# The layer end of a two-layer hybrid recurrent decoder step: three pieces of work issued at other places

## The reference

```python
h = rmsnorm(x, p['norm_w'])
proj = einsum('bld,dn->bln', h, p['w_in'])        # 1024 -> 25 chunks of 128 columns
# S5: a complex scan over time gives y, then
y = gelu(y)
y = y * sigmoid(einsum('blc,cn->bln', y, w_glu))  # the GLU: a 256 x 256 product of y itself
# HGRN2 and GLA: gated chunk scans, outputs normed per head (rmsnorm)
# RetNet: retention scan, output normed per head with its mean taken off (layernorm)
mix = concat([y_s5 * silu(s5_z), y_hg * silu(hg_z), y_gla * silu(gla_z), y_ret * silu(ret_z)])
x = x + einsum('bln,nd->bld', mix, p['w_out'])    # 1024 -> 1024
# after both layers: a final rmsnorm
```

## Time and profile before

| | us |
|---|---|
| median of three runs | 356.77 |
| lowest, highest | 356.39, 358.14 |
| the profiled execution, its own time | 357.73 |
| the profiled execution, its span | 355.9 |
| TensorE busy in the span | 333.9 (94%) |
| VectorE busy | 229.8 (65%) |
| ScalarE busy | 128.3 (36%) |

### The profile page before, as it was taken

One profiled execution on the slowest core, in us unless ns is written; L12 is line 12 of the kernel. 1 busy time (PEld: TensorE's weight loads), 2 busy tenths in 40 slices (PEclk: granted clock), 3 DMA queues, 4 the chain that ended last, 5 costly groups with the idle time before them and its releaser, 6 DMA issues.

```text
span 355.9 us, 6388 instructions
## 1 busy us (share of the span) xinstructions
PE 333.9 (94%) x2546; PEld 282.8 (79%) x2546; DVE 229.8 (65%) x481; ACT 128.3 (36%) x282; POOL 43.9 (12%) x81
## 2 busy tenths in 40 slices
PE   7899998889999999989979999999999999999991
PEld 6588876668889898769957888878888989767990
DVE  2574499986548973585559527596654897358454
ACT  4252001150780103982312620124276010596421
POOL 4028520006000002140000000000500000120000
PEclk9999999999999999899989999999999999989997
DMA  8977631232522401499805473322442433437503
GB/s 282 385 245 258 207 114 61 82 97 87 155 90 97 142 2 31 150 209 362 338 1 173 138 260 97 105 88 88 122 150 65 133 99 112 148 85 151 182 0 122
DMA packets 28012, 50.84 MB, mean 143 GB/s; under 512 B 6288, under 2 KB 6864, under 8 KB 27984
## 3 DMA queue, kind: packets, MB, share of 16 engines
q1 hardware_dynamic: 25968, 44.06, 37.3%
q0 software_dynamic: 1728, 6.29, 7.3%
q10 hardware_dynamic: 288, 0.09, 0.1%
HBM read 46.80 MB, written 3.64 MB: 142 GB/s over the span
## 4 chain that ended last, share of the span: by engine, by line
PE 68%; DVE 13%; ACT 10%; POOL 4%; issue 2%; DMA 1%; DVEq 0%; POOLq 0%; ACTq 0%
PE pr L486 39%; PE pr L759 10%; ACT u L966 4%; DVE att L1319 2%; PE wk L553 2%; DVE h L1051 2%; PE wk L675 2%; PE wk L500 2%; ACT w_lo L1027 2%; POOL lev L1556 2%; PE wk L598 1%; POOL lev L1558 1%; PE wk L566 1%; PE wk L667 1%; PE wk L613 1%
## 5 line engine op out<-in xcount | busy, mean ns | idle before, releaser
L486 PE MATMUL pr<-h,wring 128*128 128x264 f32 x768 | 184.2, 397 | 3.2 <-DVE h L1051 3.2
L486 PEld LDWEIGHTS pr<-h,wring 128*128 128x128 f32 x768 | 146.6, 194 | 31.5 <-issue 5.9
L759 PE MATMUL pr<-a_hi,w_hi 128*128 128x264 f32 x96 | 27.6, 288 | 0.0
L759 PE MATMUL pr<-a_lo,w_hi 128*128 128x264 f32 x96 | 27.2, 283 | 0.0
L759 PE MATMUL pr<-a_hi,w_lo 128*128 128x264 f32 x96 | 27.2, 283 | 0.0
L943 ACT ACTIVATE zs<-pr 128x264 f32<-128x264 f32 x16 | 6.0, 384 | 45.1 <-PE pr L486 45.0
L872 ACT ACTIVATE v<-pr 128x264 f32<-128x264 f32 x12 | 4.7, 388 | 48.2 <-PE pr L486 48.2
L860 ACT ACTIVATE h<-x 128x264 f32<-128x264 f32 x24 | 9.5, 420 | 32.7 <-DVE x L1460 30.6
L1319 DVE COPY_PREDICATED att<-masks,wk 128x512 f32<-128x512 int32 x20 | 17.6, 949 | 1.0
L759 PEld LDWEIGHTS pr<-a_hi,w_hi 128*128 128x128 f32 x96 | 18.1, 188 | 0.1
L759 PEld LDWEIGHTS pr<-a_lo,w_hi 128*128 128x128 f32 x96 | 18.1, 188 | 0.1
(11 more groups left out here) (279 smaller groups left out, 539.9 us busy)
## 6 DMA issues: line engine op xcount, KB each, us to landing
wring<-in_w_in SPq DMA_DIRECT2D x100, 256.0 KB, 3.0
wring<-in_w_out SPq DMA_DIRECT2D x20, 256.0 KB, 3.7
w_hi<-in_w_out POOLq DMA_DIRECT2D x6, 512.0 KB, 4.4
w_lo<-in_w_out POOLq DMA_DIRECT2D x6, 512.0 KB, 8.2
x<-in_xt SPq DMA_DIRECT2D x2, 528.0 KB, 4.6
out_y<-h SPq DMA_DIRECT2D x4, 264.0 KB, 2.1
s5m_t<-in_s5m SPq DMA_DIRECT2D x2, 512.0 KB, 4.9
ss<-in_hg_in SPq DMA_DIRECT2D x2, 512.0 KB, 4.0
```

The source lines that it names most:

```text
L486: mm = nc.tensor.matmul(ring_bank(layer, i)[:, 0:TT], wring[:, slot, n, :], act_in[:, k, :], start=(k == 0), stop=(k == KT - 1))
L759: mm = nc.tensor.matmul(ring_bank(layer, i)[:, 0:TT], w[:, j % WSLOTS, n, :], a[:, k, :], start=(k == 0 and p == 0), stop=(k == KT - 1 and ...
```

## The change

Four pieces, in both layers:

1. On ScalarE, tanh of the S5 gelu is issued ahead of SiLU of chunk 23 (it was behind it). On VectorE, the end of the gelu follows the first `gather_outputs`.
2. The back copies are divided: groups 0 and 1 go to VectorE, as `tensor_scalar` with factor 0.5, ahead of the second `gather_outputs`; groups 2 and 3 stay on ScalarE, behind SiLU of chunk 23. TensorE, and VectorE in `s5_mix`, wait for one more semaphore, `yg_act`.
3. On TensorE the GLU product and the two head means go ahead of chunk 24. On ScalarE tanh of the GLU product and the three negating copies go ahead of SiLU of chunk 24. The banks `pr` follow by a list, `BANK_TURN`, that gives the turns in the new order.
4. On VectorE, `head_gates` of tiles 0 to 3 goes from ahead of `center` to behind the second `square_outputs`.

```diff
+        BANK_TURN = list(range(NCH - 1)) + [NCH, NCH + 1, NCH - 1] + list(range(NCH + 2, USES))
         def ring_free(eng, layer, i):
-            i -= 3
+            i = BANK_TURN.index(i) - 3
             if i < 0:
                 layer, i = layer - 1, i + USES
+            i = BANK_TURN[i]
...
         def ring_bank(layer, i):
-            return pr[(layer * USES + i) % 3]
+            return pr[(layer * USES + BANK_TURN.index(i)) % 3]
...
             def glu_gate(layer):
                 pe.wait_ge(yg_ready, layer + 1)
+                pe.wait_ge(yg_act, layer + 1)
...
                 sample_outputs(layer, 1)
-                project(layer, NCH - 1)
                 glu_gate(layer)
                 ret_means(layer)
+                project(layer, NCH - 1)
                 head_norms(layer)
...
-            def s5_back(layer):
+            def s5_back(layer, groups):
                 act.wait_ge(yb_ready, layer + 1)
...
-                for a in range(4):
+                for a in groups:
...
-                         yg_ready if a == 3 else None)
+                         yg_act if a == groups[-1] else None)
...
                     if i == NCH - 2:
                         for n in range(2):
                             s5_evac(layer, n)
-                    if i == NCH - 1:
                         act.wait_ge(tin_ready, layer + 1)
                         step(fn(yt2, yt2, ACT.Tanh, scale=GELU_C), tanh_ready)
-                        s5_back(layer)
+                    if i == NCH - 1:
+                        s5_back(layer, (2, 3))
+                        act.wait_ge(glu_done, layer + 1)
+                        step(fn(glu[:, :, :], wk[:, 0:2, 0:TT], ACT.Tanh, scale=0.5), glu_tanh)
+                        negated_high(layer)
                     silu(layer, i)
...
-                for n in range(BY_DMA):
-                    act.wait_ge(hi_in[n], 16 * (layer + 1))
-                    step(fn(w_lo[...], w_hi[...], ACT.Copy, scale=-1.0), neg_ready)
-                act.wait_ge(glu_done, layer + 1)
-                step(fn(glu[:, :, :], wk[:, 0:2, 0:TT], ACT.Tanh, scale=0.5), glu_tanh)
                 use_logs()
...
+            def s5_back(layer, groups):        # VectorE
+                settle()
+                yv = yb.rearrange("p (t s k) -> p t s k", t=2, s=4)
+                for a in groups:
+                    for j in range(4):
+                        dst = qrt(yg, a)[:, :, 0:TP].rearrange("p t (k j) -> p t k j", j=SL)[:, :, :, j]
+                        step(ts(dst, qrt(yv, j)[:, :, a, 0:SC], 0.5, None, ALU.mult))
+                    step(ts(qrt(yg, a)[:, :, TP:TT], qrt(yv, 0)[:, :, a, SC:], 0.5, None, ALU.mult),
+                         yg_ready if a == groups[-1] else None)
...
                 s5_gelu(layer)
-                for kind in range(2):
-                    gather_outputs(layer, kind)
+                gather_outputs(layer, 0)
                 s5_gelu_end(layer)
+                s5_back(layer, (0, 1))
+                gather_outputs(layer, 1)
                 gather_outputs(layer, 2)
                 gather_samples(layer)
                 square_outputs(layer, slice(0, 4))
-                head_gates(layer, range(0, 4))
                 center(layer)
                 square_outputs(layer, slice(4, 6))
+                head_gates(layer, range(0, 4))
                 s5_mix(layer)
```

More of the change, by code:

```diff
@@ L280, in build @@
             sem(n) for n in ("gtr_evac", "sin_ready", "y_evac", "tanh_ready", "glu_tanh", "osq_ready", "ors_ready", "lb_act", "lb2_act"))
+        yg_act = sem("yg_act")
         dve_step, h_ready, t_ready, ls_ready, tree_ready, op_ready, lvl_used = (
@@ L967, in s5_back, with negated_high @@
                     step(fn(qrt(yg, a)[:, :, TP:TT], qrt(yv, 0)[:, :, a, SC:], ACT.Copy, scale=0.5),
-                         yg_ready if a == 3 else None)
+                         yg_act if a == groups[-1] else None)
+            def negated_high(layer):
+                for n in range(BY_DMA):
+                    act.wait_ge(hi_in[n], 16 * (layer + 1))
+                    step(fn(w_lo[:, 2 * n:2 * n + 2, :, :], w_hi[:, 2 * n:2 * n + 2, :, :].bitcast(F32), ACT.Copy, scale=-1.0), neg_ready)
             def s5_evac(layer, n):
@@ L1024, in _ @@
                         s5_turned(layer, range(4))
-                for n in range(BY_DMA):
-                    act.wait_ge(hi_in[n], 16 * (layer + 1))
-                    step(fn(w_lo[:, 2 * n:2 * n + 2, :, :], w_hi[:, 2 * n:2 * n + 2, :, :].bitcast(F32), ACT.Copy, scale=-1.0), neg_ready)
-                act.wait_ge(glu_done, layer + 1)
-                step(fn(glu[:, :, :], wk[:, 0:2, 0:TT], ACT.Tanh, scale=0.5), glu_tanh)
                 use_logs()
@@ L1413, in s5_gelu_end @@
                 step(stt(out=yb, in0=yt2, scalar=1.0, in1=yb, op0=ALU.add, op1=ALU.mult), yb_ready)
+            def s5_back(layer, groups):
[7 more added lines that the diff above has]
+                         yg_ready if a == groups[-1] else None)
             def s5_mix(layer):
+                dve.wait_ge(yg_act, layer + 1)
                 dve.wait_ge(glu_tanh, layer + 1)
```

## The result

The changed kernel takes 353.64 us (median of 13 runs, 351.23 to 356.90); the kernel before, in its 13 runs, 356.39 us (354.53 to 358.14). The ratio is 0.9909, 95% interval 0.9884 to 0.9933: 2.4 to 4.1 us faster. Forecast were 356.2 us and a range from 355.0 to 357.3 us. The ratio is that of the means of the fast runs: two executions of the changed kernel, 356.81 and 356.90 us, count as slow and are left out, and with them it is 0.9927.

What follows compares the result with a forecast made beforehand. TensorE, 94% busy, was taken as near its limit, with the first Ln's start deciding the layer end. Ln 0.30 us earlier in each of two layers gives 0.6 us: 356.77 to 356.2 us, range 355.0 to 357.3 us.

Steps and rivals of the forecast that it cites:

- VectorE's share: VectorE's ten back copies take 2.6 us, ending at 138.3 us, before ScalarE's half; they cost nothing.
- TensorE waits 0 to 0.2 us: Sign of being right: before the GLU product TensorE waits this long for `yg`; 0.1 us was expected.
- the same 28 records with the same 1.97 us of slow clock: TensorE's GLU product, means and chunk 24 keep their 8.43 us in the new order, ending at 151.0 us.
- the prediction's second rival: Clock falls once more at TensorE's gaps by the norms and output chunk 0: 1.7 us each, 359.6 us in both layers; 5%.
- The clock falls once less: Rival: the layer end keeps 2.4 GHz, giving 354.2 us for one layer, 352.2 us for both; 10%.
- By itself this gives nothing: Tanh of the gelu moved earlier on ScalarE gains zero before part 2, since no engine on the path uses it.
- The rule on the table load: Before Ln on ScalarE: 1.3 us taken for the load; the skill's extra drain, 2.66 us in all, would mean 358.8 us.
- It does nothing: Rival: `yg` comes 0.4 us or more after 142.48 us and the wait eats the gain, 356.8 us; 14%.
- slower: Outcome slower by more than 1.8 us, through an added slow clock in both layers, a delayed table load or mishap; 8%.
- TensorE's gap at the fourth norm: TensorE's idle time before the fourth head norm, ended by Ln, shrinks from 1.18 to about 0.8 us.
- The three times before span 1.75 us, about one such stretch.: Argument for a varying clock: the earlier kernel's spread of times is about one slow stretch at chunk 24.

Runs made afterwards that it cites:

- the run with the outputs apart: Kernel before, with the first half of the sample outputs moved ahead of the retention outputs; 355.78 us, ratio 1.0002.
- after twice: The changed kernel measured two times without further edit: 353.64 us (ratio 0.9909), then 351.64 us (ratio 0.9868).
- back copies early: Changed kernel with ScalarE's back copies of groups 2 and 3 ahead of SiLU of chunk 23; 351.68 us, ratio 0.9859.
- part 4 undone: Changed kernel with head gates of tiles 0 to 3 back ahead of `center`; 353.39 us, ratio 0.9910.
- no division: Changed kernel with all four groups of back copies on ScalarE, GLU product still ahead of chunk 24; 364.90 us, ratio 1.0228.
- Parts 1 and 2 alone: Changed kernel with chunk 24 back ahead of the GLU product and head gates back ahead of `center`; 352.98 us, ratio 0.9890.
- run without part 3: Changed kernel with chunk 24 back ahead of the GLU product and ScalarE's block behind its SiLU; 355.25 us, ratio 0.9947.
- the combined version: Changed kernel with sample outputs split, copies before SiLU 23, chunk 24 before GLU, third negating copy behind second Exp, head gates before `center` and S5 mix; 350.40 us.
- the three profiles with the two halves 2.5 us apart: First half of sample outputs ahead of retention outputs: in the kernel before (355.78 us), the changed kernel (352.21 us) and the combined version (350.40 us).

## Why the prediction was wrong

The chain through ScalarE was read rightly, the load and Ln too, and so was where the new gap would be. What was wrong is the price of TensorE's stretch ahead of the norms, and with it what the clock is worth.

- **Parts 1 and 2.** The last copy for `yg` ended at 143.00 us and the GLU product started at 143.10 us, 0.23 us after TensorE was free (142.87 us, 1.97 us behind the first sample output as before); the forecast was 0.1 (0 to 0.2). The copies began at 138.91 us, just behind the end of SiLU of chunk 23 and not 0.1 us ahead of it. VectorE's share was hidden, as forecast. That "TensorE waits 0 to 0.2 us" was off by a little; one more place for the copies (ahead of SiLU) takes the wait away.
- **"Then follow the same 28 records with the same 1.97 us of slow clock, 150.91 - 142.48 = 8.43 us."** This is the step that failed, twice over. First, 8.43 us was not TensorE's own work. In the new order the records take 6.30 us at full clock and 8.00 us with a slow stretch, so a slow stretch costs 1.70 us and not 1.97 us (the prediction's second rival had 1.7 us). In the old order they take 6.34 us at full clock and without a wait, so about 8.04 us with a slow stretch, an estimate; the other 0.39 us of the 8.43 was the wait for `yg`. It did not show, because the profile models the ends of matmuls: the row of the GLU product had no idle time, and I took chunk 24 to have ended just before it. The 0.43 us that the stretch is shorter, less 0.13 us more wait for `yg` and 0.10 us more ahead of SiLU of chunk 24 (it starts 0.20 us after the norms, forecast 0.1), turns 0.30 us a layer into 0.54 us (0.04 us of it is the forecast's rounding), the number measured in layer 0, where a slow stretch stood again.
- Second, I carried the slow stretch over as a constant. The forecast treats TensorE's time ahead of the norms as something both orders pay. But in the old order nothing of it was on the path: the chain of the earlier trace rows left TensorE at 138.11 us and came back at 153.59 us. The old order pays 15.86 us with a slow stretch and, from chunk 24 on, the same without one, as the run with the outputs apart shows (13.88 against 13.89 us). The new order pays 15.32 us with it and 13.65 us without it. Since the stretch isn't there in every layer end, the gain is 0.54 us in one and 2.22 us in another.
- **"The clock falls once less" at 10%.** The rival was listed, but as luck, the same for both kernels, and priced against the time of the new order alone. It needed no fewer slow stretches: those that do not come had given the old kernel nothing, and give the new one 1.7 us each. Two layer ends give 1.1 to 4.4 us; the measured 2.75 us between the medians lies in the middle. The table by mean clock says the same of 100 executions. A mean clock doesn't say where a slow stretch stood; in the five profiled executions with the changed kernel's order at the outputs (after twice, back copies early, part 4 undone, and no division with its own idle gap) it stood in five of ten layer ends. How many of them an execution holds stays luck, and so does the exact time within 1.1 to 4.4 us of gain.
- **"By itself this gives nothing" (part 1) and the share of part 3.** The gain was looked for in part 3. The prediction says this of part 1 alone and never prices parts 1 and 2 together; the two expectations that call their zero its forecast say more than it did. Parts 1 and 2 alone give 1.78 us a layer at full clock, part 3 0.43 us. I had computed that Ln moves by 0.30 us because chunk 24 then stands ahead of it, and did not ask what the old TensorE order would do with `yg` early.
- **The rule on the table load.** The load took 1.28 us behind a SiLU that had just read a bank, started 0.02 us after it, and Ln followed at once: no drain of 1.38 us. The Trainium skill (ScalarE: Activation LUTs, What ACT_TABLE_LOAD costs) gives 1283 ns for the load itself, and the trace agrees; what it adds for the drain doesn't show here.
- **"It does nothing" and "slower".** Neither came. The gaps of 0.85 us brought no slow stretch. A wait of 4.06 us at `yg` did: the slower rival's mechanism is real at that size.
- **TensorE's gap at the fourth norm** shrank from 1.18 to 0.85 us (forecast 0.8), with Ln at 153.00 us (forecast 152.85, in an execution that ran 0.39 us late, so 0.24 us sooner than forecast). TensorE waited for no weight transfer in that profile, and `head_mix` not for the head gates, as forecast.
- **"The three times before span 1.75 us, about one such stretch."** The spread of the kernel before isn't the clock. At one and the same mean clock of 0.979 its executions take 355.48 to 358.19 us, at 0.989 354.64 to 358.25 us. What makes these 3 us is open.

The boundary of the layers is a different matter, as is the middle of layer 0, where five profiles (outputs apart in the old order, changed kernel again, no division, back copies early, parts 1 and 2 alone) held a slow stretch near 67 us. The boundary's slow stretch (1.69 us) was in both profiles of the kernel before and in neither of the changed kernel; it also stood in the run without part 3, in the one with part 4 undone and in the combined version. So it belongs to neither order as far as these runs tell, and a part of the difference between profiles is this and not the change. Whether the time won at a layer end also makes a slow stretch rarer at the boundary stays open.

## What to carry to other kernels

Where the chain leaves an engine for a long stretch, that engine's speed in the stretch is worth nothing before the change and may be worth all of it after. So split the time between two points into the engine's own work at full speed, its slow stretches and its hidden wait before taking it over into a new order; the distance between the same starts in a run that neither waits nor slows (6.34 us) gives the first part, and a record count times the pace of clean rows elsewhere comes close (16 x 0.2225 = 3.56 us for a chunk, by 147.54 to 151.10 us, where chunk 24 behind the sample outputs takes 3.67 us). And when an engine becomes the bound, ask what makes it slow at times, and price the change with and without that.

## What the runs showed of the hardware

- A wait of TensorE need not show as idle time. Behind the sample outputs chunk 24 takes 3.67 us at full clock (142.75 to 146.42 us without part 3), so with a slow stretch about 3.67 + 1.70 = 5.37 us, an estimate. In the kernel before, the GLU product started 5.66 us after it (0.29 us more), and layer 0 lists no idle time of PE there (layer 1 lists 0.16 us). The weight loads' row shows 0.56 us:

```profile
148.14 1.63 PEld L720 LDWEIGHTS wk<-u,s5m_t 128*128 128x128 f32 x8 [0.56 <-ACT u L967]
```

- 64 very small matmul records in 2 us (two and four columns) stand ahead of every slow stretch at a layer end. That they bring it is not shown. In the three profiles with the two halves 2.5 us apart there was none in six layer ends; with the halves together it came in some layer ends and not in others, in one and the same kernel too. With an idle gap of 4.06 us after them the stretches lasted 6.83 and 10.24 us at 1.2 GHz; all other slow stretches between the first chunk and the last lasted 3.41 us.
- VectorE's four head gates took 2.63 us beside GpSimd's tensor operations and 1.70 us without them (layers 0 and 1 of the run without part 3).
- A slow stretch of 3.41 us costs dense TensorE work 1.70 us (8.00 against 6.30 us), and cost the kernel that in the new order, where TensorE is the bound of the layer end, and 0.0 us in the old one (13.89 against 13.88 us).
- `tensor_scalar` of 32 x 128 in f32 from SBUF to SBUF, with a stride of four on one side, takes VectorE 0.30 us; the same copy on ScalarE 0.45 us.
